# Attention's chunks ahead of the wide convolution's in a hybrid decoder layer, with attention's steps and the convolution's taps placed anew

## The chip, the cores and the metric

One core of one Trainium2 chip runs the whole program. The metric is device time in microseconds of one execution. Engines are named as in the profile: PE is the matrix engine, PEld its weight loads, DVE the vector engine, ACT the scalar engine, POOL is GpSimd, SP issues the weight DMAs.

## What is computed

Two layers of a decoder trunk, on 512 prompt tokens and 8 decode tokens together (520 columns, in two halves of 260). Cut to what matters here, a layer is:

```python
xn = rms_norm(x, norm_mix)
(sc_h, sc_b, sc_c, cf_a, cf_b, aq, ak, av, gq, gk, gv, gg, ga, gates) = split(xn @ w_in)
o_a = sc_b * dwconv3(sc_c * sc_h)                                  # short convolution
o_b = silu(layer_norm(dwconv31(cf_a * sigmoid(cf_b))))             # wide convolution
o_c = sliding_window_attention(rope(rms_norm(aq)), rope(rms_norm(ak)), av, caches, sinks)
o_d = rms_norm(gla(gq, gk, gv, decay(ga))) * silu(gg)
m = sum(sigmoid(gate_r) * (o_r @ w_branch[r]) for r in range(4))
x = x + m @ w_out
x = x + swiglu(rms_norm(x, norm_ffn))
```

The four branches depend on nothing but `xn`, so their output chunks can be computed in any order that respects the steps inside each branch.

## The kernel before

Activations lie transposed: channels on the 128 partitions, tokens along the row. All of `w_in` and `w_branch` is cut into output chunks of 128 channels. The list `SLOTS` gives their order: 103 slots a layer, and PE works through them one after the other. A chunk of `w_in` is 8 input tiles times 3 products (weights and activations are each split in a rounded part and a rest, `whi` and `wlo`, `xhi` and `xlo`) times 2 halves, so 48 matmuls; a branch chunk has 24. Products alternate between two accumulators, `acc`.

Around slot n each engine does, in program order:

- PE: the product of slot n, then `side(n)`, the small matrix steps that hang on this place. It starts slot n only when DVE has taken slot n-2 out of `acc` (`acc_out`) and when the weight tile's rest `wlo` is there (`lo_done`).
- DVE: `side(n)`, then the `wlo` of the tile that slot n+2 wants (line 1271), then `evac(n)`, which takes slot n out of `acc`, and then as many taps of the wide convolution as `TAPS_AT[n]` says. A tap is one multiply-add over 512 columns of one chunk (`cacc<-cfu,pr,cacc`, 31 for each of three chunks, 93 a layer).
- ACT: `side(n)`, the rounded weight part `whi`, exponentials and sigmoids.
- POOL: the wide convolution's fourth chunk alone, from when all four chunks of its input `cfu` are written: 31 taps, each a product into `ssum` (line 1728) and an add (line 1731).

The slots that matter here, before: 0 to 7 are the wide convolution's input (`cfb`, `cfa`), 8 to 13 attention's `aq` (four), `ak` and `av`, 14 to 25 the short convolution's (`sch`, `scc`, `scb`, in two halves of six), 26 to 29 four gate chunks, 30 to 33 four branch chunks, 34 to 37 gates, 38 to 41 branches, from 42 the linear attention.

Attention hangs on slots by two tables. `SATT` (17 before) begins the decode tokens' attention: DVE copies the new key and fills `qz` (lines 1339 and 1342), and PE multiplies it with the cached keys after slot 17's product (line 663). `ATT` gives eight slots for the eight groups of the prompt (4 blocks of 128 queries, two groups of heads each). At slot ATT[g] PE makes the scores (line 701), at +1 DVE masks them and finds the maximum (`prob<-m,cs`, line 1384 and three small ones) and ACT takes exponentials, at +2 DVE divides by the sum (`prob<-prob,small`) and PE transposes (line 714), at +3 PE multiplies with the values (line 688). The first block has half the keys, so its two groups cost about half.

In a `scc` slot DVE's `evac` does the whole short convolution of that chunk, nine instructions from `tmp<-acc,rstd` to the last `sct<-small,pr,sct`; below this is called a body. In a `scb` slot it multiplies the result, ACT rounds it (`ohi`) and DVE takes the rest (`olo`) first thing in the next slot's `side`.

Of the kernel before, what the change touches and what calls it, by code (L numbers as in the profile page):

```python
# [65 lines left out]
def _add(kind, *chunks):  # L66
    for c in chunks:
        SLOTS.append((kind, c))


for _p in (0, 2):
    _add("cfb", _p, _p + 1)
    _add("cfa", _p, _p + 1)
_add("aq", 0, 1, 2, 3)
_add("ak", 0)
_add("av", 0)
for _p in (0, 2):
    _add("sch", _p, _p + 1)
    _add("scc", _p, _p + 1)
# [19 lines left out]
FIRST = {}  # L99
for _n, _k in enumerate(SLOTS):  # L100
    FIRST.setdefault(_k[0], _n)
S_AQ, S_AV, S_SCH, S_GATE_A, S_GA, S_GATE_B = (FIRST[k] for k in ("aq", "av", "sch", ("gate", 0), "ga", ("gate", 1)))


TILE_OF = []
# [38 lines left out]

ATT = [S_AV + n for n in (7, 9, 11, 13, 19, 21, 24, 28)]
SATT = S_AV + 4

G_VT, G_Z, G_KDT, G_U = S_GA + 1, S_GA + 3, S_GA + 9, S_GA + 13  # L150
# [10 lines left out]
TAPS = [(c, w) for w in range(W2) for c in (0, 1)] + [(2, w) for w in range(W2)]  # L161
TAPS_AT = {}
_left = len(TAPS)
for _first, _last, _m in ((4, 7, 3), (8, 9, 4), (10, 17, 2), (20, 21, 2), (29, 29, 2), (30, 33, 1), (34, 37, 2),
                          (38, 41, 1), (42, 53, 3)):
    for _n in range(_first, _last + 1):
        TAPS_AT[_n] = min(_m, _left)
        _left -= TAPS_AT[_n]
# [54 lines left out]
def build(nc, wt, xt, gm, par, cst, glam_d, scan_d, kc, vc, scst, ccst, gst,  # L223
          yt, o_sc, o_scs, o_cc, o_ccs, o_k, o_ks, o_v, o_vs, o_g, o_gs):
    ctx = ExitStack()
    with ctx:
# [342 lines left out]
        with nc.Fori(0, DEPTH) as layer:  # L569
            with nc.Block() as block:  # L570
# [28 lines left out]
                def _(pe):  # L599
# [22 lines left out]
                    def side(n):  # L622
# [56 lines left out]
                        for g in range(NBLK * NKV):  # L679
                            blk = g // 2  # L680
                            k0 = 0 if blk else 1
                            if n == ATT[g] + 3:

# [8 lines left out]
                        for g in range(NBLK * NKV):  # L692
                            blk = g // 2
                            k0 = 0 if blk else 1
                            if n == ATT[g]:
                                if g:
# [8 lines left out]
                                ins.then_inc(s["a_s"], 1)  # L705
                            if n == ATT[g] + 2:
                                pe.wait_ge(s["a_p"], g + 1)
# [238 lines left out]
                def _(a):  # L946
                    st = Steps(a, "act_order")

                    def act(out, in_, func=ACT.Copy, name=None, **kw):
                        return st(nc.scalar.activation(out, in_, func, **kw), name)  # L950

                    def load(out, in_, name):
                        a.dma_start(out, in_).then_inc(s[name], 16)

                    def of(d):
                        n = len(d.shape)
                        v = d[bass.ds(layer, 1)]
                        names = " ".join("abcdef"[:n - 1])
                        return v.rearrange(f"z {names} -> (z a) {' '.join('bcdef'[:n - 2])}")
# [36 lines left out]
                    def side(n):  # L996
                        if n == 2:
                            a.wait_ge(s["par_in"], 16)
                            a.wait_ge(y_out, layer * (KD * 16) + 16)
                            load(vs[0:WIN - 1], of(vc), "vs_in")  # L1000
                        if n == 8:

                            a.wait_ge(s["cf_written"], KB)
                            load(of(o_cc), cfu[:, :, SEQ:SEQ + W2 - 1], "cf_out")
                            load(of(o_ccs), cfs[:, :, :, 1:W2], "cf_out")
# [4 lines left out]
                        c = n - (S_AQ + 2)  # L1010
# [24 lines left out]
                        for g in range(NBLK * NKV):  # L1035
                            blk = g // 2
                            k0 = 0 if blk else 1
                            if n == ATT[g] + 3:
                                a.wait_ge(s["a_t"], g + 1)
                                for kc_ in range(k0, 2):  # L1040
                                    act(probt[:, kc_], m4[:, 2 + kc_], name="a_tc" if kc_ == 1 else None)
                            if n == ATT[g] + 4:
                                a.wait_ge(s["a_o"], g + 1)
                                act(q[:, g % 2 * 2:g % 2 * 2 + 2, blk * P:blk * P + P],
                                    m4[:, 2, 0:2 * P].rearrange("p (h n) -> p h n", h=2), name="a_out")
                            if n == ATT[g] + 1:
                                a.wait_ge(s["a_max"], g + 1)
# [4 lines left out]
                        c = n - (ATT[-1] + 5)  # L1052
# [41 lines left out]
                        c = n - (LN_Y + 1)  # L1094
# [10 lines left out]
                        c = n - S_GATE_B  # L1105
# [54 lines left out]
                    for n, (kind, c) in enumerate(SLOTS):  # L1160
# [7 lines left out]
                        gate = isinstance(kind, tuple) and kind[0] == "gate"  # L1168
# [89 lines left out]
                def _(dve):  # L1258
                    st = Steps(dve, "vec_order")
# [27 lines left out]
                    def out_of(n, dst, name="acc_out"):  # L1287

                        dve.wait_ge(s["acc_done"], n + 1)
                        return tt(halves(dst), acc_of(n % 2), halves(rstd[:]), ALU.mult, "acc_out")  # L1290
# [15 lines left out]
                        return (tmp[:, 2], ge[:]) if p == 0 else (tmp[:, 0], tmp[:, 1])  # L1306

                    def side(n):
                        if n == 4:
                            dve.wait_ge(s["par_in"], 16)  # L1310
                        if SLOTS[n - 1][0] == "scb":
                            c = SLOTS[n - 1][1]
                            split(olo[0][:, c], sct[:, c % 2], ohi[0][:, c], "o_split", ("o_hi", c + 1))
                        if SLOTS[n - 1][0] == "gg":

                            c = SLOTS[n - 1][1]
                            dve.wait_ge(s["e_done"], exp_index[n - 1])
                            tt(gg[:, c], gg[:, c], tmp[:, c % 2], ALU.mult, "gg_done")
                        c = n - (S_AQ + 4)
# [10 lines left out]
                        c = n - (S_AQ + 2)  # L1330
# [64 lines left out]
                        c = n - (ATT[-1] + 5)  # L1395
# [66 lines left out]
                        c = n - LN_Y  # L1462
# [4 lines left out]
                        c = n - (LN_Y + 2)  # L1467
# [14 lines left out]
                        c = n - S_GATE_B  # L1482
# [40 lines left out]
                    def evac(n, kind, c):  # L1523
                        gate = isinstance(kind, tuple) and kind[0] == "gate"
                        branch = isinstance(kind, tuple) and kind[0] == "branch"
                        if n == 0:
                            dve.wait_ge(s["rstd_done"], 1)
                        if kind == "cfb":
                            out_of(n, gt[:, c % 2])
                        elif kind == "cfa":  # L1530
                            r = out_of(n, gt[:, 2 + c % 2])
                            st.need(r)
                            dve.wait_ge(s["e_done"], exp_at["cfb", c])
# [369 lines left out]
```

## Time and profile before

| | us |
|---|---|
| median of 3 runs | 2064.53 (2064.05 to 2064.55) |
| the profiled execution, its own time | 2065.61 |
| its span | 2063.8 |
| PE busy in the span | 2012.2 |
| DVE busy | 1226.2 |
| ACT busy | 781.8 |
| POOL busy | 380.7 |

The span is what the trace covers; the profiled execution took 1.8 us more than its span, and 1.1 us more than the median of the runs. Times in the rows below are in us from the start of the span. The two layers are built from one loop body, and each wait shown for the first layer has its twin some 1023.9 us later.

### The profile page before, as it was taken

Reading aid. Unit: us, or ns where it says so; the run is one execution under the profiler, and the core shown is the slowest. Engines: PE = TensorE matmul, PEld = TensorE weight load, DVE = VectorE, ACT = ScalarE, POOL = GpSimd, SP = SyncE. Lnnn points to the kernel's source line nnn. Section 1 sums busy time; section 2 is a strip of 40 time slices with the busy share of each in tenths; the row PEclk is TensorE's granted clock in tenths of the full one; section 3 lists DMA queues with packets and bytes.
Section 4 is the critical chain, followed back from the end, with each engine's and each line's share of the span. In section 5 each row is a group of like instructions: output and inputs, shape, how many; then the busy total and the mean of one; then the engine's idle time right before and its main releaser. Section 6 shows DMA issues by size and latency. Waiting matters only on the chain.

```text
span 2063.8 us, 39007 instructions
## 1 busy us (share of the span) xinstructions
PE 2012.2 (97%) x16572; PEld 1971.5 (96%) x16572; DVE 1226.2 (59%) x1667; ACT 781.8 (38%) x1209; POOL 380.7 (18%) x238
## 2 busy tenths in 40 slices
PE   6999999999999999999989999999999999999998
PEld 6999999999999999999989999999999999999998
DVE  4898668755556543355539985787455454533445
ACT  4323533553543332233233144336534334322332
POOL 0695000311103000000307940002111130000003
PEclk9999999999999999999999999999999999999999
DMA  7524522222322222222444243222223222232223
GB/s 239 98 85 83 83 77 98 83 95 83 124 82 103 82 97 92 97 82 79 141 121 80 101 63 82 93 83 87 91 82 141 86 92 92 82 101 85 99 77 128
DMA packets 70041, 199.57 MB, mean 97 GB/s; under 512 B 41555, under 2 KB 42707, under 8 KB 51409
## 3 DMA queue, kind: packets, MB, share of 16 engines
q1 hardware_dynamic: 26144, 177.50, 26.1%
q10 hardware_dynamic: 43760, 20.11, 5.7%
q8 instruction: 104, 1.70, 0.4%
q14 instruction: 33, 0.26, 0.0%
HBM read 187.42 MB, written 12.29 MB: 97 GB/s over the span
## 4 chain that ended last, share of the span: by engine, by line
PE 42%; DVE 6%; issue 1%; ACT 1%; POOL 0%; ACTq 0%; DVEq 0%; POOLq 0%
PE acc L604 40%; DVE cacc L1265 1%; DVE wlo L1271 1%; DVE q L1262 1%; DVE sct L1265 0%; ACT tmp L950 0%; PE m L701 0%; PE m L688 0%; PE m L714 0%; PE m L618 0%; DVE gt L1262 0%; DVE small L1262 0%; PE m L816 0%; PE m L788 0%; PE m L826 0%
## 5 line engine op out<-in xcount | busy, mean ns | idle before, releaser
L604 PE MATMUL acc<-xhi,wlo 128*128 128x260 f32 x3680 | 754.1, 286 | 28.7 <-PEq L567 19.4
L604 PE MATMUL acc<-xhi,whi 128*128 128x260 f32 x3680 | 743.0, 284 | 0.0
L604 PE MATMUL acc<-xlo,whi 128*128 128x260 f32 x3680 | 742.4, 283 | 0.0
L604 PEld LDWEIGHTS acc<-xhi,wlo 128*128 128x128 f32 x3680 | 571.0, 189 | 42.3 <-issue 34.6
L604 PEld LDWEIGHTS acc<-xhi,whi 128*128 128x128 f32 x3680 | 569.3, 189 | 0.0
L604 PEld LDWEIGHTS acc<-xlo,whi 128*128 128x128 f32 x3680 | 569.0, 189 | 0.0
L1271 DVE TENSOR_TENSOR wlo<-raw,whi 128x1024 fp32r<-128x1024 f32 (+3 forms) x344 | 435.7, 1275 | 36.7 <-ACT whi L967 35.3
L967 ACT ACTIVATE whi<-raw 128x1024 fp32r<-128x1024 f32 (+3 forms) x344 | 332.1, 994 | 252.7 <-PE acc L604 195.2
L950 ACT ACTIVATE gt<-gt 128x520 f32<-128x520 f32 x226 | 144.4, 639 | 214.1 <-DVE gt L1262 209.2
L1262 DVE TENSOR_TENSOR gt<-acc,rstd 128x520 f32<-128x520 f32 x80 | 55.9, 699 | 210.6 <-PE acc L604 185.6
L604 PE MATMUL acc<-hhi,whi 128*128 128x260 f32 x704 | 141.5, 282 | 0.0
L604 PE MATMUL acc<-hlo,whi 128*128 128x260 f32 x704 | 141.5, 282 | 0.0
L604 PE MATMUL acc<-hhi,wlo 128*128 128x260 f32 x704 | 141.4, 282 | 0.0
L1265 DVE SCALAR_TENSOR_TENSOR cacc<-cfu,pr,cacc 128x512 f32<-128x512 f32 x180 | 140.1, 804 | 1.6
L1772 POOL TENSOR_TENSOR tmp<-x 128x520 f32<-128x520 f32 x2 | 2.1, 1054 | 656.0 <-DVE x L1691 656.0
L1728 POOL TENSOR_SCALAR ssum<-cfu,pr 128x512 f32<-128x512 f32 x60 | 120.9, 2016 | 5.9
L1659 DVE TENSOR_TENSOR gt<-acc,rstd 128x520 f32<-128x520 f32 x44 | 30.8, 700 | 134.0 <-PE acc L604 122.8
L604 PEld LDWEIGHTS acc<-hlo,whi 128*128 128x128 f32 x704 | 108.4, 188 | 0.0
L604 PEld LDWEIGHTS acc<-hhi,wlo 128*128 128x128 f32 x704 | 108.3, 188 | 0.0
L604 PEld LDWEIGHTS acc<-hhi,whi 128*128 128x128 f32 x704 | 108.3, 188 | 0.0
L604 PE MATMUL acc<-ohi,wlo 128*128 128x260 f32 x512 | 106.7, 290 | 0.5 <-DVE gt L1262 0.5
L604 PE MATMUL acc<-ohi,whi 128*128 128x260 f32 x512 | 103.0, 283 | 0.0
(224 smaller groups left out, 2093.8 us busy)
## 6 DMA issues: line engine op xcount, KB each, us to landing
raw<-in_wt SPq DMA_DIRECT2D x142, 1024.0 KB, 4.8
raw<-in_wt SPq DMA_DIRECT2D x16, 768.0 KB, 4.3
raw<-in_wt SPq DMA_DIRECT2D x16, 640.0 KB, 3.8
x<-yt ACTq DMA_DIRECT2D x2, 2080.0 KB, 9.4
yt<-x ACTq DMA_DIRECT2D x16, 260.0 KB, 2.1
x<-in_xt SPq DMA_DIRECT2D x4, 520.0 KB, 5.0
yt<-in_xt SPq DMA_DIRECT2D x1, 2080.0 KB, 16.3
s<-in_gs ACTq DMA_DIRECT2D x4, 512.0 KB, 3.8
```

The lines of the kernel that those rows point to most:

```text
L604: ins = nc.tensor.matmul(out[:, h], a, b[:, h * TH:h * TH + TH], start=first and n == 0, stop=last and n == 2)
L950: return st(nc.scalar.activation(out, in_, func, **kw), name)
L967: nc.scalar.activation(whi[:, ts, 0:length], raw[:, e, off:off + length], ACT.Copy)\
L1262: return st(nc.vector.tensor_tensor(out, in0, in1, op), name)
L1265: return st(nc.vector.scalar_tensor_tensor(out=out, in0=in0, scalar=scalar, in1=in1, op0=op0, op1=op1), name)
L1271: nc.vector.tensor_tensor(wlo[:, ts, 0:length], raw[:, e, off:off + length], whi[:, ts, 0:length].bitcast(F32), ALU.subtract)\
L1659: nc.vector.tensor_tensor(halves(t), acc_of(0), halves(rstd[:]), ALU.mult)\
L1728: st(nc.gpsimd.tensor_scalar(ssum[:, 0:SEQ], cfu[:, c, w:w + SEQ], par_("cc", c * W2 + w), None, ALU.mult))
L1772: nc.gpsimd.tensor_tensor(tmp[:, 0], x[:, 0], x[:, 0], ALU.mult).then_inc(s["ss_sq"], 1)
```

## The change

The six attention chunks are moved ahead of the eight chunks of the wide convolution's input: slots 0 to 5 are now `aq`, `ak`, `av`, 6 to 13 are `cfb` and `cfa`, and from slot 14 on the order is as it was. `SATT` follows `av`, from 17 to 9. `ATT` goes from slots 20, 22, 24, 26, 32, 34, 37, 41 to slots 12, 14, 17, 19, 23, 25, 28, 31. The taps are dealt out anew: none before slot 10 (they began at slot 4), none in slots 16 to 18 and 22 to 24; slots 29 to 33 have 2, 3, 4, 2, 3 (they had 2, 1, 1, 1, 1), slots 34 and 35 two each, slots 36 to 50 three each, where the last tap falls (it fell in slot 53). Two waits are added ahead of writes to buffers that attention and the convolution share, and two fixed slot numbers become relative ones. No instruction is added or dropped apart from that; only order and waits change.

```diff
+_add("aq", 0, 1, 2, 3)
+_add("ak", 0)
+_add("av", 0)
 for _p in (0, 2):
     _add("cfb", _p, _p + 1)
     _add("cfa", _p, _p + 1)
-_add("aq", 0, 1, 2, 3)
-_add("ak", 0)
-_add("av", 0)
 for _p in (0, 2):
     _add("sch", _p, _p + 1)
...
-ATT = [S_AV + n for n in (7, 9, 11, 13, 19, 21, 24, 28)]
+ATT = [S_AV + n for n in (7, 9, 12, 14, 18, 20, 23, 26)]
 SATT = S_AV + 4
...
-for _first, _last, _m in ((4, 7, 3), (8, 9, 4), (10, 17, 2), (20, 21, 2), (29, 29, 2), (30, 33, 1), (34, 37, 2),
-                          (38, 41, 1), (42, 53, 3)):
+for _first, _last, _m in ((10, 11, 3), (12, 12, 2), (13, 13, 1), (14, 14, 2), (15, 15, 1), (19, 20, 2), (21, 21, 3),
...
-                        if n == 8:
+                        if n == S_CF + 8:
 
                             a.wait_ge(s["cf_written"], KB)
                             load(of(o_cc), cfu[:, :, SEQ:SEQ + W2 - 1], "cf_out")
...
-                        if n == 4:
+                        if n == S_AQ + 2:
                             dve.wait_ge(s["par_in"], 16)
...
                         if kind == "cfb":
+                            if c < 2:
+                                st.need(("qk_n", 5))
                             out_of(n, gt[:, c % 2])
                         elif kind == "cfa":
+                            if c == 0:
+                                st.need(("qk_out", 5))
                             r = out_of(n, gt[:, 2 + c % 2])
```

Three places show how the order on DVE moves. In all of them `wlo<-raw,whi` is a weight tile's rest.

The first is DVE ahead of the decode tokens' attention, before: the end of slot 16's body, that slot's two taps, then slot 17's `side`.

```order
L1265 SCALAR_TENSOR_TENSOR sct<-scu,pr,sct 128x512
L1265 SCALAR_TENSOR_TENSOR sct<-small,pr,sct 128x8
L1265 SCALAR_TENSOR_TENSOR cacc<-cfu,pr,cacc 128x512 x2
L1339 COPY kts<-kt 128x8
L1342 COPY qz<-q 64x8x4 x2
L1271 TENSOR_TENSOR wlo<-raw,whi 128x1024
```

And the same copies in the changed kernel, in slot 9, behind slot 8's `wlo` and `evac`.

```order
L1272 TENSOR_TENSOR wlo<-raw,whi 128x1024
L1263 TENSOR_TENSOR gt<-acc,rstd 128x520
L1263 TENSOR_TENSOR cfs<-gt 128x8
L1263 TENSOR_TENSOR cfu<-gt 128x512
L1340 COPY kts<-kt 128x8
L1343 COPY qz<-q 64x8x4 x2
```

What stood behind a whole body and two taps now stands behind a short evacuation.

The second is DVE behind the two `scc` slots of the short convolution's second half, before (slots 23 and 24): the end of the second body, then a first-block division by the sum.

```order
L1265 SCALAR_TENSOR_TENSOR sct<-scu,pr,sct 128x512
L1265 SCALAR_TENSOR_TENSOR sct<-small,pr,sct 128x8
L1262 TENSOR_TENSOR small<-small 128x4
L1392 RECIPROCAL small<-small 128x4
L1262 TENSOR_TENSOR prob<-prob,small 128x4x128
L1271 TENSOR_TENSOR wlo<-raw,whi 128x1024
```

In the changed kernel, behind the two bodies of slots 16 and 17 (slots 22 and 23 read alike), the steps of a full group, slots 18 and 19.

```order
L1266 SCALAR_TENSOR_TENSOR prob<-m,cs 128x512 x2
L1385 TENSOR_REDUCE small<-prob 128x4
L1263 TENSOR_TENSOR small<-small,pr 128x4
L1263 TENSOR_TENSOR small<-pr,small 128x4
L1389 TENSOR_SCALAR small<-small 128x4
L1272 TENSOR_TENSOR wlo<-raw,whi 128x1024
L1263 TENSOR_TENSOR tmp<-acc,rstd 128x520
L1263 TENSOR_TENSOR sct<-sct,tmp 128x520
L1263 TENSOR_TENSOR olo_88<-sct,ohi_86 128x520
L1263 TENSOR_TENSOR small<-small 128x4
L1393 RECIPROCAL small<-small 128x4
L1263 TENSOR_TENSOR prob<-prob,small 128x1024
```

Two bodies are now followed by the masking and the division of a group of twice the width, with slot 18's evacuation and its `olo` between.

The third is DVE in the branch slots. Before, slots 37 (its last tap group) to 39 read like this.

```order
L1265 SCALAR_TENSOR_TENSOR prob<-m,cs 128x512 x2
L1384 TENSOR_REDUCE small<-prob 128x4
L1262 TENSOR_TENSOR small<-small,pr 128x4
L1262 TENSOR_TENSOR small<-pr,small 128x4
L1388 TENSOR_SCALAR small<-small 128x4
L1271 TENSOR_TENSOR wlo<-raw,whi 128x1024
L1262 TENSOR_TENSOR mg<-acc,gt 128x520
L1265 SCALAR_TENSOR_TENSOR cacc<-cfu,pr,cacc 128x512
L1262 TENSOR_TENSOR small<-small 128x4
L1392 RECIPROCAL small<-small 128x4
L1262 TENSOR_TENSOR prob<-prob,small 128x1024
```

In the changed kernel the last group stands in slots 32 and 33, behind the evacuation and four taps of slot 31.

```order
L1266 SCALAR_TENSOR_TENSOR cacc<-cfu,pr,cacc 128x512 x4
L1266 SCALAR_TENSOR_TENSOR prob<-m,cs 128x512 x2
L1385 TENSOR_REDUCE small<-prob 128x4
L1263 TENSOR_TENSOR small<-small,pr 128x4
L1263 TENSOR_TENSOR small<-pr,small 128x4
L1389 TENSOR_SCALAR small<-small 128x4
L1272 TENSOR_TENSOR wlo<-raw,whi 128x1024
L1263 TENSOR_TENSOR mg<-acc,gt 128x520
L1266 SCALAR_TENSOR_TENSOR cacc<-cfu,pr,cacc 128x512 x2
L1263 TENSOR_TENSOR small<-small 128x4
L1393 RECIPROCAL small<-small 128x4
L1263 TENSOR_TENSOR prob<-prob,small 128x1024
```

The group itself is the same; there are four taps ahead of it and two inside it where one stood.

## Rows read from the trace of the kernel before

**Rows 1.** The page: span, and busy time by engine.
```profile
span 2063.8 us, 39007 instructions
...
PE 2012.2 (97%) x16572; PEld 1971.5 (96%) x16572; DVE 1226.2 (59%) x1667; ACT 781.8 (38%) x1209; POOL 380.7 (18%) x238
```

**Rows 2.** PE's waits: who waited for whom, us in total, times, longest.
```profile
PE m L663 <- DVE qz L1342: 7.2, 2, 3.6
PE m L714 <- DVE prob L1262: 5.5, 4, 1.7
```

**Rows 3.** Timeline of PE at slots 17 and 77: start, length, what, count, [idle before].
```profile
138.61 3.44 PE L663 MATMUL m<-kts,qz 128*64 128x128 f32 x16 [3.59 <-DVE qz L1342]
...
486.00 1.92 PE L826 MATMUL m<-s,gqz 128*16 128x128 f32 x16
```

**Rows 4.** Windows: PE, PEld, DVE, ACT, POOL busy, then PEclk, the granted clock.
```profile
138.00:142.00 4.00, 3.39 (x17) 3.06 (x17) 3.87 (x8) 0.00 (x0) 3.72 (x4) 0.61 0.21 35
```

**Rows 5.** Timeline of PE, small steps of the attention groups.
```profile
189.55 0.66 PE L714 MATMUL m<-cs,prob 128*128 128x128 f32 x4 [1.65 <-DVE prob L1262]
...
244.75 1.04 PE L714 MATMUL m<-cs,prob 128*128 128x128 f32 x8
245.71 1.13 PE L701 MATMUL m<-kt,q 64*128 64x256 f32 x8
...
275.52 1.09 PE L714 MATMUL m<-cs,prob 128*128 128x128 f32 x8 [1.11 <-DVE prob L1262]
```

**Rows 6.** Timeline of DVE, from slot 3's evacuation to slot 4's.
```profile
45.16 0.70 DVE L1262 TENSOR_TENSOR gt<-acc,rstd 128x520 f32<-128x520 f32 x1 [3.13 <-PE acc L604]
...
46.58 1.22 DVE L1271 TENSOR_TENSOR wlo<-raw,whi 128x1024 fp32r<-128x1024 f32 x1
50.92 0.70 DVE L1262 TENSOR_TENSOR gt<-acc,rstd 128x520 f32<-128x520 f32 x1 [3.13 <-PE acc L604]
```

**Rows 7.** Timeline of ACT, the first sigmoid.
```profile
33.16 1.98 ACT L950 ACTIVATE gt<-gt 128x520 f32<-128x520 f32 x3 [0.77 <-DVE gt L1262]
```

**Rows 8.** Timeline of POOL: the fourth chunk's first step, one add, the last.
```profile
69.84 3.49 POOL L1724 TENSOR_SCALAR cacc<-cfu,pr 128x512 f32<-128x512 f32 x1 [3.44 <-DVE cfu L1262]
...
78.58 1.40 POOL L1731 TENSOR_TENSOR cacc<-cacc,ssum 128x512 f32<-128x512 f32 x1
...
183.61 1.61 POOL L1731 TENSOR_TENSOR cacc<-cacc,ssum 128x512 f32<-128x512 f32 x1
```

**Rows 9.** Timeline of DVE: beside POOL's work (first four), and behind its end.
```profile
78.75 2.31 DVE L1271 TENSOR_TENSOR wlo<-raw,whi 128x1024 fp32r<-128x1024 f32 x1
...
129.57 0.69 DVE L1262 TENSOR_TENSOR tmp<-acc,rstd 128x520 f32<-128x520 f32 x1
...
135.69 1.42 DVE L1265 SCALAR_TENSOR_TENSOR cacc<-cfu,pr,cacc 128x512 f32<-128x512 f32 x2
...
183.98 0.69 DVE L1262 TENSOR_TENSOR tmp<-acc,rstd 128x520 f32<-128x520 f32 x1
...
188.39 0.16 DVE L1262 TENSOR_TENSOR small<-small 128x4 f32<-128x4 f32 x1
...
192.68 0.70 DVE L1262 TENSOR_TENSOR olo<-sct,ohi 128x520 fp32r<-128x520 f32 x1 [0.70 <-ACT ohi L950]
```

**Rows 10.** Timeline of DVE in slots 38 and 39.
```profile
268.51 1.29 DVE L1265 SCALAR_TENSOR_TENSOR prob<-m,cs 128x512 f32<-128x512 f32 x2
...
271.43 1.22 DVE L1271 TENSOR_TENSOR wlo<-raw,whi 128x1024 fp32r<-128x1024 f32 x1
272.57 0.69 DVE L1262 TENSOR_TENSOR mg<-acc,gt 128x520 f32<-128x520 f32 x1
273.18 0.74 DVE L1265 SCALAR_TENSOR_TENSOR cacc<-cfu,pr,cacc 128x512 f32<-128x512 f32 x1
273.84 0.15 DVE L1262 TENSOR_TENSOR small<-small 128x4 f32<-128x4 f32 x1
...
274.24 1.22 DVE L1262 TENSOR_TENSOR prob<-prob,small 128x1024 f32<-128x1024 f32 x1
```

More of the change, by code:

```diff
@@ L101 @@
     FIRST.setdefault(_k[0], _n)
-S_AQ, S_AV, S_SCH, S_GATE_A, S_GA, S_GATE_B = (FIRST[k] for k in ("aq", "av", "sch", ("gate", 0), "ga", ("gate", 1)))
+S_AQ, S_AV, S_CF, S_SCH, S_GATE_A, S_GA, S_GATE_B = (FIRST[k] for k in ("aq", "av", "cfb", "sch", ("gate", 0), "ga", ("gate", 1)))
 TILE_OF = []
@@ L163 @@
 _left = len(TAPS)
-for _first, _last, _m in ((4, 7, 3), (8, 9, 4), (10, 17, 2), (20, 21, 2), (29, 29, 2), (30, 33, 1), (34, 37, 2),
-                          (38, 41, 1), (42, 53, 3)):
+for _first, _last, _m in ((10, 11, 3), (12, 12, 2), (13, 13, 1), (14, 14, 2), (15, 15, 1), (19, 20, 2), (21, 21, 3),
+                          (25, 26, 2), (27, 27, 3), (28, 28, 4), (29, 29, 2), (30, 30, 3), (31, 31, 4), (32, 32, 2),
+                          (33, 33, 3), (34, 35, 2), (36, 53, 3)):
     for _n in range(_first, _last + 1):
```

## The prediction

> **What bounds the kernel now.** I read the page first: PE is busy for 2012 of 2064 us [rows 1], and the change neither adds nor drops a product, so it can only move the moments at which PE stands still or runs slowly. The view of PE's waits says which those are [rows 2]: PE waits 7.2 us for the `qz` copies, once a layer, and 5.5 us for the attention's divided `prob`, twice a layer. Then the timeline of PE at each of them. At slot 17 it stands idle for 3.59 us, and the 16 matmuls behind the wait take 3.44 us, where 16 of the same width take 1.92 elsewhere [rows 3]; the window there has a granted clock of 0.61 on average [rows 4], that is, the lower of the two levels for much of it. At slots 24 and 39 it idles 1.65 and 1.11 us, and what follows takes its usual time (8 transposes 1.09 against 1.04) [rows 5]. So the trace prices a stall in two parts, the idle time, and, behind 3.59 us but not behind 1.65, a fall of the clock.
>
> A product of 48 matmuls takes 5.8 us, the distance between two evacuations with no step between them (45.16 to 50.92, both ended by PE) [rows 6]; a branch product has half the matmuls, 2.9.
>
> Why DVE is late at slot 17: it does a body, two taps and then the copies. The body starts at 129.57 and ends at 135.69, 6.1 us. The same nine instructions from 183.98 to 188.39 take 4.4 us [rows 9]. The first lies inside POOL's convolution (69.84 to 185.2), the second nearly behind it [rows 8]. DVE's `wlo`, too, takes 2.31 us at 78.75, where POOL's add runs from 78.58 to 79.98, against 1.22 elsewhere [rows 6, 8, 9]. DVE therefore pays for POOL's work wherever it is laid.
>
> The Trainium skill (SBUF — State Buffer, Who interferes with whom) has this as an exclusive lock: a DVE instruction with two inputs in SBUF and a GpSimd one that reads SBUF shut each other out for the whole instruction. By that rule a step that meets an add is held for up to all of it, 1.4 us by row, while the masking, whose scores come from PSUM, is never held. Held as badly as that, the two waits booked below at 2.7 and 2.6 would come out near 4.2, and the sum 6 us higher; the row of 78.75 agrees with the rule, the unheld `wlo` steps elsewhere show that it doesn't strike each time.
>
> **What the change removes.** In slot 9 the copies stand behind a `cfa` evacuation of 1.4 us (45.16 to 46.58) [rows 6] and need 1.6 (135.69 to 138.61 less two taps) [rows 3, 9]. They are done 3.3 us behind slot 8's end, PE asks for them after slot 9's product, 5.8 us and a small step behind it. POOL is idle there. The wait goes, and the slow matmuls with it: 3.6 and about 1.6 (3.44 against 1.92), 5.2 in all. The waits at slots 24 and 39 lose their places: with the restart about 1.8 and 1.3. Together 8.3 us a layer.
>
> **What it adds**, place by place, with DVE's steps by the rows: evacuation 0.6, tap 0.66, `wlo` 1.13, `scb` evacuation with its multiply 1.4, masking of a full group 2.9 (268.51 to 271.43), division 1.6 (273.84 to the end of 274.24's) [rows 10]; an `olo` right behind its evacuation waits 0.7 for ACT and takes 0.6 [rows 9].
>
> Slot 1: the squares for the norm of `aq` are now needed after the second product. In both orders slot 0 is evacuated late, since `rstd` is; ACT then begins at 33.16 [rows 7] and one pass takes a third of 1.98. PE ends slot 1 at about 33.4. Wait 0.45 a layer. Before, nobody asked for anything here.
>
> Slots 16 to 19. Count from the end of slot 16's product. PE: 0.5 for 4 transposes, product 5.8, value product and scores 1.7 (by 1.04 and 1.13, half and whole) [rows 5], two products 11.6, and a tenth or two per restart: it asks for group 2's division at 19.8. DVE: starts at 0.2; body 5.9; `wlo` 1.5; body 5.9; masking 2.9; `wlo` 1.5; slot 18's evacuation 1.4; `olo` 1.3; division 1.6; 0.3 for blocked steps: 22.5. Wait 2.7. POOL works through all of it: it now starts when slot 13 is written, not slot 7, so behind six more products and attention's small steps, at 110 to 120, and its 115 us [rows 8] end at 225 to 235, near slot 29. The two unknowns are body and `wlo` beside POOL. If both bodies take the free 4.4 and `wlo` 1.13, the second body waits for slot 17's product (6.5) instead, and the sum is 19.9: no wait. If both take 6.1 and `wlo` 2.2, it is 24: wait 4.2. I take 5.9 and 1.5 because the place is like 129.57, wholly beside POOL.
>
> Slots 22 to 25 repeat this with group 4. PE has a full value product more at the start: wait 2.6, same bounds.
>
> Slot 30. From the end of slot 29's product DVE does 0.2 + 0.6 + two taps 1.3 + division 1.6 = 3.7; PE has a branch product of 2.9 only. Wait 0.75.
>
> Slots 31 to 33. Same origin. PE: 3.75, transposes 0.8 to 1.0, product: 7.5; value product and scores 2.2, product 12.7, product 15.7: it asks for the last division. DVE: at 3.7 `wlo` 1.1, evacuation 0.6, three taps 2.0 = 7.4; waits for slot 31 until 7.7; evacuation 0.6, four taps 2.65, masking 2.9, `wlo` 1.1, evacuation 0.6, two taps 1.3, division 1.6 = 18.5. Wait 2.85. POOL is done or nearly, so this sum has little play: 2.5 to 3.5.
>
> Slots 38 to 41 had one tap each and now have three, with an `olo` in two of them: DVE 4.4, 3.2, 3.9, 4.1 against 2.9 of PE. PE may lead by two slots; slot 42 starts about 0.45 late (0 to 1.5). Slots 42 to 50: 0.6 + 1.1 + 2.4 = 4.1 against 5.8, covered; slot 47's extra 4 us is caught up in two slots.
>
> At nothing: the two added waits, since DVE itself wrote what they wait for, earlier in its order. The moved DMAs: the convolution-state stores (two issues on ACT) go to slot 14, where ACT's next work is one slot off; the eight issues of the new value rows hold ACT in slot 9 while PE has a product and 16 matmuls, and the cover is 6 us deep. The weight queue on SP follows `wlo` and is passed by nothing. The shorter tap tail (slot 50, not 53) frees DVE ahead of the linear attention, where PE hardly waited.
>
> **The sum.** Added waits 0.45 + 2.7 + 2.6 + 0.75 + 2.85 + 0.45 = 9.8, and 0.3 to 0.4 of restarts, 10.1 a layer, against 8.3 removed: +1.8 a layer, +3.6 in all. To it come falls of the clock: three waits a layer of 2.6 to 2.85 lie between the 1.65 us that left it alone and the 3.59 that did not; each fall costs 1.6. Midway between the two rows I count half of six, +4.8. The sum is +8.4 against the profiled execution's span of 2063.8 (own time 2065.6), so 2074.0 for such an execution and, from the median of 2064.5, 2073.
>
> **Rivals.** (A) The forecast, 2069 to 2080, chance 0.52.
>
> (B) Faster. DVE's bodies beside POOL come out near the free 4.4: the waits at slots 19 and 25 fall away together. Then 4.8 added against 8.3, -7 in all, with at most one fall at slot 33: about 2059. For it: DVE has fewer taps ahead of these slots than before, and half of the masking comes from PSUM. Against: two whole bodies (6.1 each) stood beside POOL before. It decides where two bodies and two `wlo` together stay under about 13 us (the forecast has 14.8). Chance 0.24.
>
> (C) No change. The waits come as counted and the clock never falls behind them: +3.6, 2068, within 0.2% (4.1 us), which is about what a measurement of this kernel tells from no change. The Trainium skill (TensorE: Matmul & The Clock Gate, Why this matters for your kernels) warns only of longer idle gaps than the ones I count; by that the sum would end here. Also here: only one of the two waits at 19 and 25. Chance 0.18.
>
> (D) More than forecast: blocked at every step, waits of 4 at slots 19 and 25, all six falls and more, about 2084. Chance 0.06.
>
> The range goes from B's 2059 to A's upper end 2080 and leaves out D and the better part of B. Faster 0.24 (B), same 0.21 (C and the lowest edge of A), slower 0.55 (the rest).
>
> **What would show it.** PE's wait for `qz` is gone, and the matmuls of line 663's step take 1.9 us. PE waits for `prob` at four places a layer, by 2.5 to 3 us at slots 19, 25 and 33 and below 1 at slot 30, and for ACT's square by 0.45 at slot 1. POOL's convolution runs from about 118 to 230, and the bodies of slots 16, 17, 22, 23 take 5.4 to 6.1. The granted clock is low for some 3 us behind about half of the long waits. I am wrong if the bodies take under 5 us, if the wait at slot 33 is under 2 (then my count of DVE's taps against branch products is off), or if a new wait stands where I booked nothing, above all at ACT in slots 9 to 14.

## The result, and the profile after

The changed kernel takes 2085.89 us in the median of 4 runs (2081.45 to 2087.77); the kernel before took 2064.54 in 4 runs beside it. The ratio is 1.0099, 95% interval 1.0086 to 1.0112: slower by 21.4 us. I had forecast slower, but by 8.4, and 2085.9 lies above the upper end of my range, 2080. The profiled execution took 2085.99 us, 20.4 more than that of before.

The page, with the same columns as [rows 1]:

```profile
span 2084.2 us, 39011 instructions
...
PE 2021.4 (97%) x16572; PEld 1978.1 (95%) x16572; DVE 1221.9 (59%) x1667; ACT 782.4 (38%) x1209; POOL 374.4 (18%) x238
```

PE has the same 16572 instructions and is "busy" for 9.2 us longer. Matmuls at a lower clock count as busy, so about half of the loss is hidden in that number. PE's waits, beside [rows 2]:

```profile
PE m L715 <- DVE prob L1263: 22.5, 8, 3.9
...
PE acc L605 <- DVE mg L1263: 1.2, 2, 0.6
PE m L702 <- issue: 0.6, 1, 0.6
```

The wait for `qz` is gone, as forecast, and the one for `prob` has grown from 5.5 to 22.5 us. The timeline of PE shows where (slots 19, 25, 28, 30, 33 and 42 of the first layer, then 19, 25 and 33 of the second):

```profile
160.92 1.14 PE L715 MATMUL m<-cs,prob 128*128 128x128 f32 x8 [3.92 <-DVE prob L1263]
...
207.32 1.97 PE L715 MATMUL m<-cs,prob 128*128 128x128 f32 x8 [3.42 <-DVE prob L1263]
...
233.87 0.70 PE L702 MATMUL m<-kt,q 64*128 64x256 f32 x4 [0.58 <-issue]
...
244.17 1.09 PE L715 MATMUL m<-cs,prob 128*128 128x128 f32 x8 [0.77 <-DVE prob L1263]
...
259.10 1.09 PE L715 MATMUL m<-cs,prob 128*128 128x128 f32 x8 [2.95 <-DVE prob L1263]
...
297.17 0.51 PE L605 MATMUL acc<-xhi,wlo 128*128 128x260 f32 x2 [0.59 <-DVE mg L1263]
...
1193.24 1.97 PE L715 MATMUL m<-cs,prob 128*128 128x128 f32 x8 [3.91 <-DVE prob L1263]
...
1241.28 1.97 PE L715 MATMUL m<-cs,prob 128*128 128x128 f32 x8 [3.77 <-DVE prob L1263]
...
1292.34 1.97 PE L715 MATMUL m<-cs,prob 128*128 128x128 f32 x8 [2.95 <-DVE prob L1263]
```

The eight transposes take 1.09 us at full clock and 1.97 where the clock is low, so the length of the step behind a wait tells the clock at once. The windows (columns as in [rows 4]; PEclk is the third number from the end) give the low stretches:

```profile
161.90:165.20 3.30, 3.30 (x14) 2.40 (x14) 3.27 (x5) 1.61 (x3) 3.15 (x2) 0.50 0.59 191
206.30:213.00 6.70, 5.68 (x24) 4.53 (x25) 6.67 (x8) 1.72 (x3) 6.52 (x3) 0.50 0.51 153
256.00:262.00 6.00, 3.05 (x27) 2.90 (x26) 5.93 (x10) 4.32 (x9) 0.00 (x0) 1.00 0.14 22
1192.70:1199.40 6.70, 6.16 (x26) 5.01 (x27) 6.67 (x9) 1.61 (x3) 6.52 (x3) 0.50 0.44 159
1240.50:1247.20 6.70, 5.92 (x25) 4.77 (x26) 6.67 (x9) 1.72 (x3) 6.52 (x3) 0.50 0.55 157
1291.70:1295.00 3.30, 2.66 (x13) 2.67 (x14) 3.30 (x5) 0.74 (x3) 0.00 (x0) 0.50 0.22 30
```

The granted clock falls to 0.5 (1.2 GHz) behind all four waits at slots 19 and 25, three times for 6.8 us and once for 3.4, and behind one of the two at slot 33. Behind the other, at 256 to 262 us, it stays at 1.00. In the kernel before it was low for 3.4 us at slot 17 of each layer.

A fall needs no wait, though. In both kernels the clock is also low for 3.4 us once a layer, in the linear attention near slot 80, where PE has had no idle time for over 40 us. In the kernel before (the last line is a window, its columns as above):

```profile
481.06 1.94 PE L816 MATMUL m<-vbd,tmp 8*64 8x512 f32 x8
...
491.08 1.94 PE L816 MATMUL m<-vbd,tmp 8*64 8x512 f32 x8
...
493.80:497.30 3.50, 3.50 (x19) 3.50 (x18) 2.57 (x7) 0.00 (x0) 0.00 (x0) 0.51 0.55 229
```

Three steps of 1.9 us with small operands, these two and the one at 486.00 [rows 3], stand in the 13 us ahead of it; that they cause it isn't shown. The stretch from the first of them (481.06) to the wait at 525.69 takes 44.64 us with such a fall and 43.12 without one, so one costs 1.5. It comes in all four layers of these two executions and in 9 of 26 over all thirteen, and it cancels in the comparison here.

Why DVE is late at slot 19, beside [rows 9]: its timeline from slot 16's body to slot 19's division.

```profile
137.50 0.70 DVE L1263 TENSOR_TENSOR tmp<-acc,rstd 128x520 f32<-128x520 f32 x1 [2.94 <-PE acc L605]
...
141.05 1.26 DVE L1266 SCALAR_TENSOR_TENSOR sct<-small,pr,sct 128x8 f32<-128x8 f32 x1
...
144.78 0.69 DVE L1263 TENSOR_TENSOR tmp<-acc,rstd 128x520 f32<-128x520 f32 x1
...
150.88 1.29 DVE L1266 SCALAR_TENSOR_TENSOR prob<-m,cs 128x512 f32<-128x512 f32 x2
...
154.07 1.22 DVE L1272 TENSOR_TENSOR wlo<-raw,whi 128x1024 fp32r<-128x1024 f32 x1
...
155.93 1.08 DVE L1263 TENSOR_TENSOR sct<-sct,tmp 128x520 f32<-128x520 f32 x1
157.88 0.70 DVE L1263 TENSOR_TENSOR olo<-sct,ohi 128x520 fp32r<-128x520 f32 x1 [0.87 <-ACT ohi L951]
158.49 0.15 DVE L1263 TENSOR_TENSOR small<-small 128x4 f32<-128x4 f32 x1
...
158.90 1.96 DVE L1263 TENSOR_TENSOR prob<-prob,small 128x1024 f32<-128x1024 f32 x1
```

DVE waits 2.94 us for slot 16's product and from there works without a break, but for 0.87 us in which it waits for ACT, until 160.86, the end of `prob`. PE had asked at 157.00. POOL's convolution runs from 119.8 to 233.2, through all of it; two of its steps:

```profile
119.79 1.19 POOL L1729 TENSOR_SCALAR cacc<-cfu,pr 128x512 f32<-128x512 f32 x1 [56.40 <-DVE cfu L1263]
...
231.92 1.27 POOL L1736 TENSOR_TENSOR cacc<-cacc,ssum 128x512 f32<-128x512 f32 x1
```

Ahead of slot 16, DVE has time to spare that it didn't have in the kernel before. Its timeline in slots 10 to 12:

```profile
97.97 0.70 DVE L1263 TENSOR_TENSOR gt<-acc,rstd 128x520 f32<-128x520 f32 x1 [3.88 <-PE acc L605]
...
103.73 0.70 DVE L1263 TENSOR_TENSOR gt<-acc,rstd 128x520 f32<-128x520 f32 x1 [1.79 <-PE acc L605]
...
109.91 0.70 DVE L1263 TENSOR_TENSOR gt<-acc,rstd 128x520 f32<-128x520 f32 x1 [2.22 <-PE acc L605]
```

It idles 3.9, 1.8 and 2.2 us there, while slots 30 to 33 are overloaded with taps.

### The profile page after: what moved, and what is told of

Same layout as the page of the kernel before. It is cut to its first block, busy times and chain, and to the rows that moved or that the text cites. A ratio compares the mean times of both kernels' runs of the same rounds, so it can differ in the third digit from the quotient of the medians.

```text
span 2084.2 us, 39011 instructions
## 1 busy us (share of the span) xinstructions
PE 2021.4 (97%) x16572; PEld 1978.1 (95%) x16572; DVE 1221.9 (59%) x1667; ACT 782.4 (38%) x1209; POOL 374.4 (18%) x238
## 4 chain that ended last, share of the span: by engine, by line
PE 45%; DVE 3%; issue 1%; ACT 1%; POOL 0%; POOLq 0%; DVEq 0%
PE acc L605 42%; DVE sct L1266 0%; PE m L715 0%; DVE cacc L1266 0%; PE m L619 0%; DVE prob L1263 0%; PE m L702 0%; DVE wlo L1272 0%; PE m L689 0%; PE m L649 0%; PE m L638 0%; ACT prob L951 0%; DVE small L1263 0%; DVE prob L1266 0%; PE m L817 0%
## 5 line engine op out<-in xcount | busy, mean ns | idle before, releaser
L1272 DVE TENSOR_TENSOR wlo<-raw,whi 128x1024 fp32r<-128x1024 f32 (+3 forms) x344 | 428.7, 1255 | 35.2 <-ACT whi L968 33.8
L1733 POOL TENSOR_SCALAR ssum<-cfu,pr 128x512 f32<-128x512 f32 x60 | 125.4, 2090 | 5.9
```

The source lines that it names most:

```text
L1272: nc.vector.tensor_tensor(wlo[:, ts, 0:length], raw[:, e, off:off + length], whi[:, ts, 0:length].bitcast(F32), ALU.subtract)\
L1733: st(nc.gpsimd.tensor_scalar(ssum[:, 0:SEQ], cfu[:, c, w:w + SEQ], par_("cc", c * W2 + w), None, ALU.mult))
```

## The experiments

Two accounts stood at the start. The first: all the loss is where DVE is late at slots 19, 25, 30, 33 and 42, and in the slow clock behind these waits. The second: something of the new order itself is dear, POOL's convolution beside the attention's full groups above all. All "times saved" below are against the changed kernel's 2085.9 or before's 2064.5.

**Fewer taps at the branch slots.**

```diff
-(29, 29, 2), (30, 30, 3), (31, 31, 4), (32, 32, 2), (33, 33, 3), (34, 35, 2), (36, 53, 3)
+(29, 29, 0), (30, 32, 1), (33, 33, 3), (34, 35, 5), (36, 37, 3), (38, 38, 2), (39, 41, 1), (42, 53, 3)
```

> The changed kernel with ten taps a layer taken out of slots 29 to 42's run-up (slots 29 to 33 have 0, 1, 1, 1, 3 in place of 2, 3, 4, 2, 3; slots 38 to 41 have 2, 1, 1, 1 in place of 3 each; slots 34 and 35 have five each), so that the last falls in slot 53 again. Theory: the waits at slots 30, 33 and 42 are nothing but DVE's taps against branch products (0.8, 2.95 and 0.6 to 1.2 us, with the slow clock behind slot 33 in the second layer), so all three vanish, 5.2 to 6 us a layer, and nothing new comes: 2074.5 us, 11 to 12 us under the changed kernel; the waits at slots 19 and 25 stay at 3.4 to 3.9. Rival: the taps only move the lateness, DVE comes late in slots 42 to 55 or in the linear attention behind them (before's tail, to slot 53, had small waits there), and no more than half is won: 2080 or more.

Measured 2078.66 us (2076.78 to 2079.49), ratio to before 1.0067 (1.0051 to 1.0082): 7.2 saved, not 11. The waits at slot 42 went, those at slot 33 shrank from 2.95 to 1.11 and had no slow clock behind them. But an irregular one at slot 28 of the first layer was 1.42 us in this execution, one of 1.29 stood at slot 30 of the second (0.79 in the changed kernel), and 0.72 us a layer came back at slot 58. Both accounts had a part: the place is right, the gain was counted too high.

**Groups 2 to 6 one slot later.**

```diff
-ATT = [S_AV + n for n in (7, 9, 12, 14, 18, 20, 23, 26)]
+ATT = [S_AV + n for n in (7, 9, 13, 15, 19, 21, 23, 26)]
-(19, 20, 2), (21, 21, 3), (25, 26, 2), (27, 27, 3), (28, 28, 4)
+(20, 20, 2), (21, 21, 3), (26, 26, 3), (27, 27, 2), (28, 28, 4)
```

> The changed kernel with groups 2 to 6 of the prompt's attention begun one slot later (slots 18, 20, 24, 26, 28 in place of 17, 19, 23, 25, 28), so that PE asks for groups 2 and 4's division behind slots 20 and 26, and with the taps of slots 19 and 25 moved behind it. Theory: at slots 19 and 25 DVE is late because two bodies, a masking and a division stand in three products; with one product more DVE has 24.6 us of work where PE asks after some 25.5, the two waits go and the slow clock behind them: 5.1 + 0.65 and 5.5 + 0.8 us in the first layer, 5.95 + 1.1 and 5.8 + 0.9 in the second by the trace of the changed kernel, 25 us in all, so about 2061 us. Rival: DVE works at its limit through slots 16 to 28, and the waits come back at slots 20, 22, 26 or 28 with about half their size: 2073 or more.

Measured 2082.64 us (2080.45 to 2086.22), ratio 1.0081 (1.0066 to 1.0096): 3.3 saved where I had expected 25. The waits only moved, to 2.83 us at slot 20 of both layers, and 3.45 and 4.62 at slot 26. My theory of this edit fell, and the rival, which had the waits come back, was nearer.

**Both edits.** Its tables are those two, with four taps in slots 42 to 45.

> Both edits together on the changed kernel (groups 2 to 6 later and the taps out of slots 29 to 42's run-up; slots 42 to 45 take four taps each). Theory: the gains add, since the places are apart: 25 + 11.5 us off the changed kernel's 2085.9, 2049 to 2050, which is 14 to 15 us (0.7%) below the kernel before, about what the three waits removed from it held (16.6). Rival: the order with attention first is costlier as such (attention's steps lie denser on DVE while POOL convolves), so that it ends no better than the kernel before, 2062 to 2068.

Measured 2075.67 us (2072.71 to 2078.17), ratio 1.0049 (1.0036 to 1.0063). The two gains do add (7.2 + 3.3, 10.2 measured), but each was smaller than I had counted, so the sum is not the 2049 expected and is still 10 us behind before. DVE's timeline in slot 20 of this kernel shows why one more product of PE's, 5.8 us, bought only 1.1:

```profile
159.54 1.07 DVE L1264 TENSOR_TENSOR sct<-sct,tmp 128x520 f32<-128x520 f32 x1
161.65 0.70 DVE L1264 TENSOR_TENSOR olo<-sct,ohi 128x520 fp32r<-128x520 f32 x1 [1.04 <-ACT ohi L952]
162.27 1.23 DVE L1264 TENSOR_TENSOR small<-small 128x4 f32<-128x4 f32 x1
...
163.75 1.59 DVE L1264 TENSOR_TENSOR prob<-prob,small 128x1024 f32<-128x1024 f32 x1
```

The added slot is a `scb` slot. It brings an evacuation, a multiply of 1.07, a wait for ACT of 1.04 and an `olo` of 0.70 to DVE, and a 4-column add that takes 0.15 elsewhere takes 1.23 here, beside POOL's work. A later place helps only if the slots that it jumps are cheap for the engine that is late.

**The kernel before with two taps fewer ahead of the copies.**

```diff
-(10, 17, 2), (20, 21, 2)
+(10, 15, 2), (17, 18, 2), (20, 21, 2)
```

> The kernel before with the two taps of slot 16, which stand ahead of the decode tokens' copies, moved to slot 18. The copies are then 1.3 us earlier and the wait at slot 17 is 2.3 us in place of 3.59. Theory (the clock falls behind an idle time near or above 3 us): the 16 matmuls behind it take 1.9 us, not 3.4, and each layer wins 1.3 + 1.5: 5.5 us in all, 2059 us. Rival (the fall comes behind any stall of some length, 2.3 us too): 2.6 us in all, 2062 us, with the granted clock low for some 3 us behind 132 to 140 us as before.

Measured 2067.08 us (2066.32 to 2069.28), ratio 1.0011 (1.0001 to 1.0020): nothing won, and a trace of a loss. Its waits of PE:

```profile
PE m L669 <- DVE sprob L1357: 6.5, 2, 3.2
PE m L714 <- DVE prob L1262: 5.8, 4, 2.0
PE m L663 <- DVE qz L1342: 3.2, 2, 1.6
```

The wait for `qz` fell to 1.6, but a new one of 3.23 us appeared two slots on, for the decode tokens' softmax, and the clock fell behind that in both layers. With it PE's waits in the attention come to 15.4 us, against 12.7 before the edit, so the move made the stalls longer, not shorter. The clock fell, too, behind a wait of only 2.01 us at slot 24 of the first layer. That speaks against the theory, which wanted about 3 us, and rather for the rival.

**POOL's convolution cut,** in the changed kernel and in the one before. Both leave out 29 of the fourth chunk's 31 taps.

```diff
-                    for w in range(1, W2):
+                    for w in range(1, 2):
```

> The changed kernel with POOL's chunk of the wide convolution cut to 2 of its 31 taps, so that chunk of the output leaves out 29 taps. Everything DVE does in slots 16 to 29 is then free of POOL's convolution. Contention theory (rival B of the prediction put the condition there): bodies take 4.4 us in place of 6.1, wlo 1.13 to 1.2 and the division 1.6, so the wait at slot 19 falls from 3.9 to 0 to 0.6 and that at 25 from 3.4 to 3.8 to about the same; the waits at 30 and 33, which lie behind POOL's end, stay at 0.8 and 2.95. With the slow clock gone behind 19 and 25 that is 23 to 25 us: 2062 us. Rival (DVE's own amount of work in three products is too large, held or not): waits of 2 us or more stay at 19 and 25, 2072 or more.

> The kernel before with the same cut of POOL's chunk (29 of 31 taps left out of that chunk). Contention theory: the body ahead of the decode tokens' copies takes 4.4 us in place of 6.1 and the wait at slot 17 falls from 3.6 to about 1.5 with no slow clock behind it; slot 24's falls from 1.65 to 0 to 1 (its first body lies beside POOL's last adds); 39's stays at 1.1. That is 3.6 + 1 us a layer, 8 to 9 in all: 2056 us, so that the changed kernel's loss to before shrinks from 21 us to some 6 under the same cut. Rival: before gains as much as after does, and the distance stays near 20 us: POOL is then no part of the difference.

Measured: the changed kernel 2063.32 us (2060.11 to 2066.65), the one before 2050.33 (2049.91 to 2051.50). So POOL's work costs the changed kernel 22.6 us and before 14.2, and the distance between them shrinks from 21.4 to 13.0: some 8 us of the difference are POOL's. DVE in slots 16 and 19 of the changed kernel with the cut:

```profile
136.70 0.70 DVE L1263 TENSOR_TENSOR tmp<-acc,rstd 128x520 f32<-128x520 f32 x1 [3.02 <-PE acc L605]
...
139.57 0.22 DVE L1266 SCALAR_TENSOR_TENSOR sct<-small,pr,sct 128x8 f32<-128x8 f32 x1
...
140.75 1.22 DVE L1272 TENSOR_TENSOR wlo<-raw,whi 128x1024 fp32r<-128x1024 f32 x1
...
154.68 1.23 DVE L1263 TENSOR_TENSOR prob<-prob,small 128x1024 f32<-128x1024 f32 x1
```

and its waits of PE:

```profile
PE m L715 <- DVE prob L1263: 8.1, 6, 3.0
PE m L702 <- issue: 2.2, 1, 2.2
```

A body takes 4.05 us (136.70 to 140.75) where it took 6.1, its 8-column step 0.22 for 1.26, the division 1.23 for 1.96. The wait at slot 19 is gone, that at slot 25 is 0.33; those at slots 30 and 33 (0.79 and 2.95) and at slot 42 (0.59) stay within 0.02. That separates the two kinds of wait: those at 19 and 25 need POOL's work, those at 30, 33 and 42 don't, and the run with fewer taps shortened or removed the latter in the first layer. POOL's work alone doesn't make the first two either: the next two runs keep it and bring such waits down to 2.0 us and then to 0.33 by the tables. The body of 4.4 us that my prediction took for free was itself partly held. In the kernel before the wait at slot 17 fell to nothing, more than the 1.5 I had left it.

**Both tables laid by DVE's idle time.** The order of slots is that of the changed kernel.

```diff
-ATT = [S_AV + n for n in (7, 9, 12, 14, 18, 20, 23, 26)]
+ATT = [S_AV + n for n in (7, 9, 14, 20, 22, 28, 30, 32)]
...
+(9, 12, 4), (13, 14, 2), (15, 15, 3), (19, 20, 1), (21, 21, 4), (26, 26, 2),
+(27, 28, 3), (29, 33, 2), (34, 34, 3), (35, 36, 4), (39, 41, 1), (42, 53, 3)
```

> The changed kernel's order of slots, with both tables laid by where DVE has idle time in its trace. No masking or division of a full group stands in slots 15 to 19 or 22 to 26 (the bodies and the scb slots behind them) nor in the branch slots 30 to 33: the groups start at slots 12, 14, 19, 25, 27, 33, 35, 37. The taps begin at slot 9 with four a slot (DVE idles 1.3 to 3.9 us in each of slots 10 to 16 of the changed kernel), 23 of them ahead of slot 16 in place of 12, and end in slot 52. Theory (the order of slots costs nothing by itself, the tables do, since two bodies, a masking, two scb slots with their olo and a division don't fit in three or four products): the waits at 19, 25, 30, 33 and 42 all go, none over 1 us takes their place, and with them the slow clock: a layer's mix is 578 to 581 us (586.8 before, 596.5 after), 2048 to 2054 us. Rival: something of the order itself (POOL's convolution beside attention's full groups, or DVE short of time as a whole) brings waits of 2 us or more back at other places, and it ends at 2062 or more.

Measured 2057.99 us (2052.95 to 2059.83), ratio 0.9962 (0.9949 to 0.9976): faster than both kernels, and 4 us above the range expected. Waits of 1.09 (slot 21) and 2.0 us (slot 29) are there in both layers, and behind the second the clock fell in one layer of two.

**Five more taps away from these two.**

```diff
-(19, 20, 1), (21, 21, 4), (26, 26, 2), (27, 28, 3), (29, 33, 2)
+(21, 21, 4), (26, 27, 2), (28, 28, 1), (29, 33, 2)
...
-(42, 53, 3)
+(42, 45, 4), (46, 53, 3)
```

> The kernel of the run before with its tables laid by DVE's idle time, and with five more taps taken from ahead of its two remaining waits of over 1 us (slots 19 and 20 none, slots 27 and 28 two and one in place of three each; slots 42 to 45 take four in place of three, so that the last falls in slot 53). Theory: each tap is 0.7 us, so the wait at slot 21 (1.09) goes by two taps and the one at slot 29 (2.0) by three, and the fall of the clock behind the second goes too: 3 us a layer and 1.7 once, 7 us under that kernel, 2050 to 2052. Rival: DVE is so full in slots 16 to 29 that what held it there was not the taps but steps held by POOL, and taps bunched in slots 42 to 45 bring small waits of their own: no more than 2 us are won, 2056 or more.

Measured 2047.97 us (2046.79 to 2050.45), ratio 0.9925 (0.9911 to 0.9939). This table's last tap falls in slot 52, by its counts, not in 53 as expected. PE's waits, without those of the start, of the layers' border and of the norms, come to one line, and the windows over the attention of both layers show what is left of idle time:

```profile
PE m L715 <- DVE prob L1263: 1.2, 4, 0.3
```

```profile
100.00:400.00 300.00, 299.35 (x2454) 288.91 (x2452) 249.28 (x360) 122.96 (x224) 125.99 (x71) 1.00 0.38 89
1130.00:1400.00 270.00, 269.34 (x2205) 259.52 (x2205) 226.48 (x322) 108.60 (x205) 113.64 (x64) 1.00 0.39 87
```

The changed kernel, in the same two windows:

```profile
100.00:400.00 300.00, 287.64 (x2316) 275.55 (x2315) 239.45 (x351) 110.21 (x207) 112.80 (x64) 0.98 0.35 82
1130.00:1400.00 270.00, 257.86 (x2062) 246.79 (x2061) 217.50 (x316) 93.80 (x182) 110.01 (x64) 0.97 0.36 83
```

PE's idle time there falls from 24.5 us to 1.3 and the granted clock returns to 1.00. The kernel is 16.6 us faster than before (2064.56 beside it), by the new order and its tables together, and 38 faster than the changed kernel, from which it differs by the two tables alone. It does POOL's whole convolution beside DVE.

**The old order with taps moved only.**

```diff
-(10, 17, 2), (20, 21, 2), (29, 29, 2)
+(10, 13, 2), (20, 21, 2), (27, 27, 4), (28, 28, 4), (29, 29, 2)
```

> The kernel before, its order of slots and its table of groups untouched, with only the eight taps of slots 14 to 17 moved to slots 27 and 28, where DVE idles 1.8 to 5.9 us. Theory: the loss at slot 17 lies in the two taps ahead of the copies and the two behind the next body, so the wait for the copies falls from 3.6 to 1.6 us, the one for the decode tokens' softmax that took its place when only slot 16's taps moved (3.2) stays under 1, and no slow clock follows: 5.2 less 2.2, 3 us a layer, 2058 to 2060. That would say that as much is to be had in the old order by the tap table alone as the new order gives with both tables laid anew. Rival: the old order can't have it, since the copies stand behind a whole body there, and taps moved only bring waits elsewhere (slot 19, slots 28 to 30): within 2 us of the kernel before.

Measured 2062.06 us (2059.22 to 2067.09), ratio 0.9990 (0.9981 to 0.9999): 2.5 saved. Its waits:

```profile
PE m L714 <- DVE prob L1262: 8.1, 4, 2.9
PE m L663 <- DVE qz L1342: 3.1, 2, 1.5
PE m L669 <- DVE sprob L1357: 2.1, 2, 1.1
```

The first two came as expected (1.5 and 1.1), but the wait at slot 24 grew from 1.65 to 2.9. Neither statement holds whole: a little is to be had in the old order by taps, not what the new order gives. Its table of groups wasn't laid anew, so how far the old order could go stays open.

**The changed kernel twice more.** There is no edit.

> The changed kernel once more, unaltered, for a second profiled execution. In the profiles so far no fall of the clock came behind waits up to 1.65 us, one came behind each of 3.2 us and more, and behind those of 2.8 to 2.95 us it came in half of the cases. Theory (the waits are set by the program and the same each time; whether and for how long the clock falls behind one near 3 us is not): waits of 3.9, 3.4 to 3.8 and 2.95 us at slots 19, 25 and 33 as before to 0.1 us, falls behind the first two each time, and a different pattern of lengths (3.41 or 6.83 us) and behind slot 33, with a span that moves by some 1.7 us for each 3.41 us of low clock. Rival (the fall is set by the instructions ahead of the wait): the same pattern as in the first profile, low behind slots 19, 25 (twice the length), 19, 25 and 33 of the second layer.

> A third profiled execution of the changed kernel, unaltered. The same as for the second: if the theory holds, all three agree in the waits and no two in the low stretches behind them.

They took 2088.60 and 2085.66 us. The waits at slots 19 (3.92 and 3.93) and 33 (2.94 and 2.95) repeat to 0.02; that at slot 25 is 3.25 to 3.47, against 3.42 and 3.77 at first. The slow clock doesn't repeat. Windows of the second execution behind slot 33, both layers:

```profile
260.10:266.60 6.50, 5.72 (x27) 5.72 (x28) 5.59 (x7) 2.26 (x4) 0.00 (x0) 0.50 0.47 161
1297.70:1300.90 3.20, 3.20 (x17) 3.20 (x17) 3.20 (x5) 1.67 (x3) 0.00 (x0) 0.50 0.78 246
```

Here the low stretch behind the same 2.95 us is 6.8 us long in the first layer, where the first execution had none; in the third execution it is 3.4 in both. So it isn't fixed by the instructions ahead of the wait, and the rival is out. Part of my theory is too: the waits at slots 27 to 30 did change between the three executions (up to 1.78 at slot 28 of the first layer, 0.8 to 2.6 at slot 30 of the second).

## Why the prediction was wrong

**What the change removes: right.** The `qz` wait is gone and the 16 products (line 664 now) have a median of 273 ns each; the waits at 24 and 39 are gone. The best version bears out the size as well: with hardly a wait put in their place, its 103 slots take 577.7 and 577.1 us in the two layers, where before took 586.8 and 586.9. That is 18.9 us less; 3.0 of it are two falls of the clock in the linear attention, which only before's profiled execution had. The other 15.9 stand against twice 8.3, 16.6. That the medians differ by 16.6 to the tenth is chance.

**Where the added waits stand: right.** Slots 19, 25, 30, 33, 42 were named and all have one. Slot 30 was booked at 0.75 and took 0.77 to 0.79, slot 33 at 2.85 and took 2.95, slot 42 at 0.45 and took 0.59. At slot 1 the 0.45 did not come (0.33 in the first layer of the version with both tables laid anew). Slot 28 had 0.58 where I had nothing.

**Slots 19 and 25: mis-sized.** I booked 2.7 and 2.6; they took 3.92 and 3.91, 3.42 and 3.77. The term I had bounded with care was good: two bodies and two `wlo` took 14.5 us against 14.8, and PE asked at 19.7 against 19.8. The error is in the steps that I booked at their free price although POOL runs beside them: the masking took 3.2 for 2.9, the multiply 1.1 for 0.7, the division with its two small steps 2.4 for 1.6 (158.49 to 160.86), and the `olo`'s wait for ACT 0.9 for 0.7. My 0.3 "for blocked steps" stood for 1.7 of these. With POOL cut the division takes 1.23 (1.96 with POOL), the multiply 0.70 (1.08) and the masking 2.9, so POOL's work is the cause there. The masking's two wide steps, which read the scores from PSUM, take 1.29 together with POOL or without; the loss is in one add on 4 columns, 0.42 for 0.16. The wait for ACT is not POOL's: it is 1.25 with the cut. The Trainium skill (SBUF — State Buffer, Who interferes with whom) has DVE steps with two inputs in SBUF shut out for the whole of a GpSimd instruction that reads SBUF; the 8-column step of 1.26 us, 0.22 with the cut, agrees.

Two bounds were also added up wrong, without changing the forecast: with free bodies my terms give 19.5, not 19.9 (the run with POOL cut has 19.4), and with all held 24.3, not 24.

All waits of both layers together, by the timeline: 24.2 us against 12.7 before, 11.5 more; booked were 6.9 more (twice 9.8, less 12.7). That leaves 4.6 of the error.

**The step that failed: "Midway between the two rows I count half of six, +4.8".** Both factors were wrong. Five of the six waits had a fall, and three of the five lasted 6.8 us, not 3.4. The mixing stage, the 103 slots, grew from 586.8 and 586.9 us to 596.5 and 597.4, by 20.2 us (the falls in the linear attention are in both); less 11.5 of waits, 8.7 are the slow clock and restarts, where I had a net 1.6 (4.8 less the 3.2 of before's two). That is 7 of the error, more than all waits; with 4.6 and the 1.1 us by which before's profiled execution lay above its median, it comes to 12.7 of the 12.9 between 2073 and 2085.9. The price of 1.6 a fall was read from one wait, 3.59 us, with its twin, and I took it for a constant. Over the thirteen profiled executions, waits of 1 us or more with the layers' border left out, the granted clock fell like this:

| wait of PE, us | waits | with a low stretch behind |
|---|---|---|
| 1.05 to 1.65 | 26 | 0 |
| 1.78 to 2.59 | 8 | 5 |
| 2.83 to 2.95 | 16 | 10 |
| 3.23 to 4.62 | 24 | 23, ten of them 6.8 us long |

The Trainium skill (TensorE: Matmul & The Clock Gate, Why this matters for your kernels), which I used for rival C, would have left the clock alone behind the second and third groups; 15 of 24 fell, so the measurement decides against it here.

**The rivals.** (B), faster, had its condition right: two bodies and two `wlo` under 13 us; they took 14.5, and with POOL cut 10.5 (twice 4.05 and twice 1.2), where the waits at 19 and 25 fell to nothing and to 0.33. (C) lost by the clock. (D), 2084 with a chance of 0.06, is nearly what happened: waits of 3.4 to 3.9 at slots 19 and 25, and five of the six falls. Its waits were in my own upper bound of 4.2, and its chance was too small, because I let the midpoint of an unknown stand for the likeliest value.

**What stays open.** What decides whether the clock falls behind a wait of 2 to 3 us, and for how long, and why it falls in some layers of the linear attention without a wait. How far the old order could go with both tables laid anew. And the stall at slots 27 and 28 of the first layer (below).

## What to carry to other kernels

A stall of the matrix engine has a second price, and it isn't proportional: here nothing behind waits up to 1.65 us, in some cases a stretch at half clock behind 1.8 to 3 us, and nearly always one, of 3.4 or 6.8 us, from 3.2 us up. So the first thing to try is to cut long stalls into short ones or none. When an order of work is changed, the tables of what hangs on it must be laid by the idle time that the new trace shows, slot by slot and for the late engine: the same order gave 2086, 2058 and 2048 us with three tables. And a step booked in the shadow of a competing engine is to be booked at its held price, small steps too.

## What was not expected of the hardware

An instruction on 4 or 8 columns can be held as long as a wide one: 1.23 us for 0.15 and 1.26 for 0.22, each beside POOL's convolution (the 1024-column division lost 0.73). For the second the run with POOL cut shows the cause.

In the first layer of four of these kernels PE stands still near slots 27 or 28 in the middle of a run of instructions, with no wait written there: between the fourth and fifth score product 0.58 us in the changed kernel (233.87 above), 1.42 and 2.24 in two experiments, 1.29 ahead of a transpose and 1.78 inside a product in the two repeats (the first of them has a second one, 0.61, 10 us on). The profile names "issue". It comes between 221 and 235 us of the span and isn't there in the best version, nor in any run of the old order; in the run with only groups 2 to 6 a slot later, one of 0.7 stood at slot 29 of either layer. Its cause wasn't tried.

The same kernel spread over 6.3 us in four runs (2081.45 to 2087.77) where the kernel before spread over 0.9 (over 3.1 in the 15 runs beside the first experiments). The three profiled executions had 27.3, 30.7 and 20.5 us of low clock in the attention, and the waits themselves hardly differed: stalls of the length that decides over the clock make a kernel's time less repeatable.
